# Retention and gated linear attention in one phase, with heads on row quarters of TensorE

## The reference

```
mod = silu(c) @ w_mod + b_mod;  shift, scale, gate = split(mod)
h = rms_norm(x, pre_gain) * (1 + scale) + shift
proj = h @ w_in                      # 3088 columns: attention, retention, gated linear attention (GLA)
r: retention, 4 heads of 64, chunks of 128 tokens
   sc = (q k^T) * dmask;  out = sc v + (q*q_decay) state;  state = chunk_decay*state + (k*k_decay)^T v
g: GLA, 4 heads, key width 32, value width 64, chunks of 64 tokens
   log_a = log_sigmoid(ga @ gate_w + gate_b) / 16;  b = cumsum(log_a) in the chunk
   sc[i,j] = sum_d q[i,d] k[j,d] exp(b[i,d]-b[j,d]) for j <= i
   out = sc v + (q*exp(b)) state;  state = exp(b_last)*state + (k*exp(b_last-b))^T v
r, g: rms_norm over each head, times silu of their gate columns
y = [attention, r, g] @ w_out;  x = x + gate * rms_norm(y, post_gain)
```

## Time and profile before

| what | before |
|---|---|
| median of 3 runs | 2690.21 us (2686.27 to 2691.15) |
| the profiled execution's own time | 2677.06 us |
| its span, first to last instruction | 2675.3 us |
| PE busy, share of the span | 90% |
| DVE, ACT, POOL busy | 51%, 32%, 40% |
| mean granted TensorE clock | 0.968 of full speed |

### The profile page before, as it was taken

One profiled execution on the slowest core, in us unless ns is written; L12 is line 12 of the kernel. 1 busy time (PEld: TensorE's weight loads), 2 busy tenths in 40 slices (PEclk: granted clock), 3 DMA queues, 4 the chain that ended last, 5 costly groups with the idle time before them and its releaser, 6 DMA issues.

```text
span 2675.3 us, 33460 instructions
## 1 busy us (share of the span) xinstructions
PE 2412.1 (90%) x13114; PEld 1993.8 (75%) x13114; DVE 1362.1 (51%) x2043; ACT 851.6 (32%) x1624; POOL 1076.0 (40%) x793
## 2 busy tenths in 40 slices
PE   3889689988689988888899999999899899999998
PEld 3777467777467865667799998989778667788886
DVE  4885654794654965547753352313479673210112
ACT  2224113214114156563422121211421784322222
POOL 1433326333326233232444242433544343655454
PEclk9999899999899999999999999999999999999999
DMA  7541013440022420002332232324153001222222
GB/s 247 169 146 37 1 56 91 153 155 5 1 64 65 150 56 1 1 9 91 111 103 79 83 107 87 103 67 130 36 185 98 17 1 40 63 98 99 95 95 79
DMA packets 147733, 218.95 MB, mean 82 GB/s; under 512 B 18485, under 2 KB 71125, under 8 KB 147449
## 3 DMA queue, kind: packets, MB, share of 16 engines
q1 hardware_dynamic: 147576, 216.82, 25.2%
HBM read 214.69 MB, written 2.10 MB: 81 GB/s over the span
## 4 chain that ended last, share of the span: by engine, by line
PE 51%; DVE 3%; ACT 2%; POOL 1%; issue 1%; DMA 0%; ACTq 0%; DVEq 0%; POOLq 0%; SPq 0%
PE ps L306 13%; PE ps L307 13%; PE ps L308 13%; PE ps L983 4%; PE ps L1011 3%; PE ps L1033 1%; PE ps L1030 1%; POOL h_transposed L560 1%; PE ps L1272 1%; PE ps L393 1%; DVE x_tokens L842 0%; PE ps L572 0%; DVE mod_acc_aux L366 0%; ACT att_probs_lat L1071 0%; PE ps L1267 0%
## 5 line engine op out<-in xcount | busy, mean ns | idle before, releaser
L295 POOL TENSOR_TENSOR w_lo<-w_raw,w_hi 128x1024 fp32r<-128x1024 f32 (+3 forms) x252 | 590.8, 2346 | 995.7 <-ACT w_hi L288 995.6
L288 ACT ACTIVATE w_hi<-w_raw 128x1024 fp32r<-128x1024 f32 (+3 forms) x252 | 255.7, 1016 | 1167.9 <-PE ps L308 983.8
L306 PE MATMUL ps<-w_hi,h_transposed 128*128 128x512 f32 (+3 forms) x1088 | 418.1, 384 | 57.0 <-POOL w_lo L295 26.5
L307 PE MATMUL ps<-w_lo,h_transposed 128*128 128x512 f32 (+3 forms) x1088 | 409.2, 376 | 0.0
L308 PE MATMUL ps<-w_hi,h_transposed 128*128 128x512 f32 (+3 forms) x1088 | 408.9, 376 | 0.0
L306 PE MATMUL ps<-h_transposed,w_hi 128*128 128x384 f32 (+1 forms) x1056 | 374.7, 355 | 8.1 <-POOL h_transposed L560 6.5
L307 PE MATMUL ps<-h_transposed,w_hi 128*128 128x384 f32 (+1 forms) x1056 | 373.9, 354 | 0.0
L308 PE MATMUL ps<-h_transposed,w_lo 128*128 128x384 f32 (+1 forms) x1056 | 373.9, 354 | 0.0
L366 DVE SCALAR_TENSOR_TENSOR mod_acc_aux<-w_raw,c_act,mod_acc_aux 128x512 f32<-128x512 f32 x280 | 283.4, 1037 | 41.5 <-DMA w_raw<-in_w_mod_dram 19.1
L306 PEld LDWEIGHTS ps<-w_hi,h_transposed 128*128 128x128 f32 x1088 | 213.3, 196 | 103.0 <-POOL w_lo L295 31.1
L1465 DVE TENSOR_TENSOR ffn_full<-ps,ffn_silu 128x768 f32<-128x768 f32 (+1 forms) x44 | 34.2, 819 | 430.8 <-PE ps L308 430.8
(11 more groups left out here) (312 smaller groups left out, 3634.3 us busy)
## 6 DMA issues: line engine op xcount, KB each, us to landing
w_raw<-in_ada_w_dram SPq DMA_DIRECT2D x96, 512.0 KB, 3.8
w_raw<-in_ffn_w_in_dram SPq DMA_DIRECT2D x88, 512.0 KB, 3.5
w_raw<-in_w_mod_dram SPq DMA_DIRECT2D x48, 512.0 KB, 4.5
w_raw<-in_ffn_w_out_dram SPq DMA_DIRECT2D x44, 512.0 KB, 3.5
w_raw<-in_w_in_dram SPq DMA_DIRECT2D x40, 512.0 KB, 4.2
w_raw<-in_w_out_dram SPq DMA_DIRECT2D x16, 512.0 KB, 4.9
w_raw<-in_od_w_in_dram SPq DMA_DIRECT2D x16, 512.0 KB, 3.9
mod_gain<-in_norm_g_dram SPq DMA_DIRECT2D x16, 256.0 KB, 3.9
```

The costliest lines, as they stand in the source:

```text
L288: act.activation(w_hi[:, i % 2, 0:k * n], w_raw[:, u % 4, 0:k * n], ACT.Copy).then_inc(w_hi_ready.sem, 1)
L295: pool.tensor_tensor(w_lo[:, i % 2, 0:k * n], w_raw[:, u % 4, 0:k * n], w_hi[:, i % 2, 0:k * n].bitcast(F32), ALU.subtract).then_inc(w_lo_ ...
L306: pe.matmul(acc, left[0], right[0], start=start, stop=False)
L307: pe.matmul(acc, left[0], right[1], start=False, stop=False)
```

## The change

- `Modulation`: x is loaded after the first job; a job's gain is loaded behind its fourth transfer; squares, roots, scales and the turns of six of the eight column tiles of x stand inside `Modulation`, between the turns of jobs 1 and 2; the barrier of its own for x is gone. The constants are loaded inside the w_in `Linear`, behind its second weight transfer.
- `Linear` with w_in: the rotary steps of tiles 0 and 1 stay in chunks 2 and 4, those of tiles 2 and 3 go to chunks 3 and 5.
- The decayed q and k of retention are made in the `Pieces` phase ahead of attention: 8 more transposes, two masked copies on DVE, four products on POOL.
- The 19 phases become one, `Memories`, with semaphores between single steps and one barrier at its end. Score banks 0 to 3 belong one to each head; banks 4 to 6 are used in turn by all other products. GLA's scores use rows 32h to 32h+31 of the array for head h (`tile_position`), in two halves of two heads. A level has only the later tokens as targets, so 256 columns for all four tiles instead of 512 for each; q and k are multiplied for half of the tokens; the copies take 256 columns a head. What stood in phases behind the levels (decays, updates, states, the sums of squares of retention) is put between the levels (`beside_level`). SP loads the next constants and weights when the last level's q and k are made.

```diff
-                if q == 2 and self.gain is not None:
+                u = ring_slot(sp, "mod")
+                sp.dma_start(w_raw[:, u % 4, :]...)
+                if q == 3 and self.gain is not None:
...
+                for t in range(XT):
+                    self.norm.turn(pe, t, range(6), None, t == XT - 1)
+                for job in self.jobs[2:]:
+                    job.turn(pe)
...
+            linear.beside["dve"] = {2: [rotate_columns(0, AQ, AV, 1, (0, 1))], 3: [rotate_columns(0, AQ, AV, 1, (2, 3))],
+                                    4: [rotate_columns(1, RQ, RV, 3, (0, 1))], 5: [rotate_columns(1, RQ, RV, 3, (2, 3))]}
...
+            def level_scores(self, pe, l, half):
+                if half == 0:
+                    self.wait(pe, g_ql, l + 1)
+                    self.wait(pe, g_kl, l + 1)
+                self.wait(pe, g_cp, 2 * l + half + 1)
+                for t in range(XT):
+                    for h in (2 * half, 2 * half + 1):
+                        rows = slice(32 * h, 32 * h + 32)
+                        ins = pe.matmul(ps[:, h, 64 * t:64 * t + 64], g_k[rows, l % 2, tok(t)], g_q[rows, l % 2, 64 * t:64 * t + 64],
+                                        start=True, stop=True, tile_position=(32 * h, 0))
+                ins.then_inc(g_mm.sem, 1)
...
+            def tensor(self, pe):
+                pe.matmul(self.bank(self.Z), gate_w[:, :], gaT[:, :], start=True, stop=True).then_inc(mem_made.sem, 1)
+                self.own_scores(pe, 0)
+                self.own_scores(pe, 1)
+                self.wait(pe, mem_cleared, 3)
+                for t in range(XT):
+                    self.retained(pe, t)
+                log_tok = self.open(pe, self.LOG)
+                self.wait(pe, gate_log, 1)
...
+                for t in range(XT):
+                    self.retention_out(pe, t)
+                keep_clock(pe, 2)
+                for l in range(len(LEVELS)):
+                    for half in range(2):
+                        self.level_scores(pe, l, half)
+                    if l == 0:
...
+                    if l == 1:
+                        self.update(pe, self.UPD)
+                        self.update(pe, self.UPD + 1)
...
+                    if l >= 3:
+                        keep_clock(pe, 2)
+                for t in range(XT):
+                    self.gated_out(pe, t)
+                keep_clock(pe, 16)
...
+            def beside_level(self, dve, step):
+                if step == 0: ...   # distance to the chunk's end
+                if step == 1: ...   # g_qe = gqT * f_in
+                if step == 2: ...   # g_kd = gkT * f_out
+                if step in (3, 4): ...   # keep two updates each
+                if step == 5: ...   # seven state steps
+                if step == 6: ...   # squares and sums of retention
...
+            # DVE, vector(): gate_min; keep_retained 0, 1; place_own 0, 1; log_a; keep_retained 2, 3; ret_s;
+            # then for step in range(8): distance(step), q(step-1), place(step-2, both halves), beside_level(step);
+            # then head_gate and head_sums of both results
...
+            # ACT, scalar(): gate abs, exp, ln; keep LOG, SUMS; f_in, gla_decay; keep RET_OUT 0 to 3;
+            # factor(0); f_out; factor(1), (2); keep KD; factor(3) to (5); keep OUT 0 to 3
```

More of the change, by code:

```diff
@@ L470, in __init__ @@
                 self.prime = prime
-                self.host, self.added, self.ahead = None, None, []
+                self.host, self.added, self.ahead, self.beside = None, None, [], None
                 self.T = XT + (CT if with_ctx else 0)
@@ L548, in gpsimd @@
             def gpsimd(self, pool):
-                if self.added is None:
+                if self.added is None and not self.beside:
                     for t in range(self.T):
@@ L1752, in layer_one, with rotate_columns @@
             linear = schedule[-1]
-            def rotate_columns(which, c0, c1, chunk):
+            def rotate_columns(which, c0, c1, chunk, tiles):
                 def step(eng):
@@ L1757, in step @@
                     linear.wait_copied(eng, chunk)
-                    for t in range(XT):
+                    for t in tiles:
                         x = P1[:, t, c0:c1]
@@ new lines, in update @@
+            def update(self, pe, g):
+                par, two = (g - self.UPD) // 2, (g - self.UPD) % 2
+                rows = slice(GLA_C * par, GLA_C * par + GLA_C)
+                acc = self.open(pe, g)
+                if g == self.UPD:
+                    self.wait_kept(pe, self.KD)
+                for i, t in enumerate((2 * two, 2 * two + 1)):
+                    ins = pe.matmul(acc[:, i * 256:(i + 1) * 256], g_kdt[rows, t, :], P1[rows, t, GV:GV + 256], start=True, stop=True)
+                ins.then_inc(mem_made.sem, 1)
@@ new lines, in place_own @@
+            def place_own(self, dve, half):
+                mask = c1t("levels")[:, 6 * P:7 * P].bitcast(U32).unsqueeze(1).to_broadcast([P, XT, P])
+                self.wait(dve, g_mm, half + 1)
+                if half == 0:
+                    self.wait(dve, mem_cleared, 1)
+                for h in (2 * half, 2 * half + 1):
+                    v = lambda z: z.rearrange("p (t n) -> p t n", n=P)
+                    ins = dve.copy_predicated(v(gla_a[:, h, :]), mask, v(ps[:, h, :]))
+                ins.then_inc(g_cp.sem, 1)
@@ L1989, in vector @@
+                        dve.tensor_tensor(g_q[:, l % 2].rearrange("p (b n) -> p b n", n=s), later(gqT[:, :]), later(g_exp[:, l % 2]), ALU.mult)\
                            .then_inc(g_ql.sem, 1)
[L1990 to L1999 removed]
@@ L2001, in gpsimd @@
-            def gpsimd(self, pool):
-                for step in range(len(LEVELS) + 1):
-                    l = step
-                    if l < len(LEVELS):
-                        s = LEVELS[l]
+                    if step >= 2:
+                        self.place(dve, step - 2, 0)
+                        self.place(dve, step - 2, 1)
+                    self.beside_level(dve, step)
+                self.wait(dve, g_cp, 2 * n + 2)
+                dve.wait_ge(rstd_ready.sem, self.r0 + 1)
@@ new lines, in vector @@
+                self.head_gate(dve, 0, RQ, RG, range(0, 2))
+                for two in range(2):
+                    self.wait_kept(dve, self.OUT + 2 * two + 1)
+                    ins = self.head_sums(dve, 1, GQ, range(2 * two, 2 * two + 2))
+                dve_s.chain(ins)
+                self.head_means(dve, 1)
+                self.head_gate(dve, 0, RQ, RG, range(2, XT))
+                dve.wait_ge(rstd_ready.sem, self.r0 + 2)
+                self.wait(dve, gains_ready, 1)
+                self.head_gate(dve, 1, GQ, GG, range(XT))
```

503 lines of the change are left out of this document (311 added, 192 removed).

## The result

The changed kernel took 2602.06 us (median of 4 runs, 2599.96 to 2604.27) against 2689.59 us: ratio 0.9677, 95% interval 0.9661 to 0.9692, or 87.5 us less. Faster, inside the range, 22 us above the forecast of 2580. Its profiled execution took 2599.96 us with a span of 2598.2.

What follows compares the result with a forecast made beforehand. No engine was full; steps waiting for each other over 19 barriers bound the rewritten stretches. Phases -86, pieces +2.4, start -14.5 and w_in -12 gave -110 from the 2690 median: 2580 us, range 2556 to 2616.

Steps and rivals of the forecast that it cites:

- phases: Retention and GLA stretch, end of attention to turn of mixed rows: 66 us against 109.1 a layer, 86 less in all.
- start: Before the first w_in product: earlier jobs and row work in their shadow save 14.5 us (10 to 17).
- w_in: Two w_in products: half the rotary work leaves chunks where DVE has a job, -7 and -5, together -12 us.
- One more us for TensorE's clock: In the retention and GLA phase: 1 us a layer added because PE idles 2 to 3 us several times.
- rival 1: PE at 1.2 GHz through most of the retention and GLA phase: +16 us a layer, 2612 us; chance 0.18.
- to level 0: From the barrier behind attention through log, summed logs, retention outputs and first exponential: level 0 begins at 20.6 us.
- levels: From level 0 to the last copy: DVE issues 26.0 us of work plus about 2.4 of waits, ending at 49.
- to the turn: After the last copy: GLA outputs 6.5, squares 2.1, POOL's root 3.34, eight steps 3.4, sinks and barrier 0.5 us.
- rival 2: Strided predicated copies or PE quarters in the levels cost as before: +7 us a layer, 2594 us; chance 0.14.
- Quarters side by side: In the levels, passes in different PE rows run side by side: half a level takes 0.9 us, otherwise 1.8.
- rival 3: Start and w_in products give only half their forecast gain: +13 us, 2593 us; chance 0.11.
- Rival 4: Strided predicated copies and products pay for each piece, making the kernel slower: at 35 ns 2705 us; chance 0.02.

Runs made afterwards that it cites:

- experiment 4: Kernel before with only the new start (x after first job, gains later, rows turned beside the jobs, constants in the first product): 2673.87 us, ratio 0.9939.
- experiment 3: Kernel before with only the rotary steps of tiles 2 and 3 moved to chunks 3 and 5 of w_in: 2681.7 us, ratio 0.9979.
- experiment 1: Changed kernel plus 256-column fillers: 8 before level 0's turns of decayed keys, 2 after levels 1 and 2, 5 instead of 2 after levels 3 to 5: 2582.79 us.
- experiment 12: Kernel of experiment 1 with each filler behind level 0 and later as four 64-column matmuls on all 128 rows: 2658.27 us, ratio 0.9881.
- experiments 9: Kernel of experiment 1 reordered, five fillers in the wait for retention states, retention outputs and key turns spread over levels 0 and 1 without fillers between: 2591.92 us.
- experiment 11: Reordered kernel of experiments 9 with more 256-column fillers ahead of level 0, behind the third and fourth retention outputs and levels 1 and 2: 2575.66 us, ratio 0.9588.
- experiment 6: Changed kernel with only eight 256-column fillers added ahead of the turns of the decayed keys in level 0: 2594.03 us, ratio 0.9656.

## Why the prediction was right, and where it was not

Sign and order came out; the saving was 0.8 of what I forecast. One of the signs of being wrong that I had named was met: the clock in the phase is 0.66, below 0.75. Term by term, with the second profile of before as the usual one:

| Term | Forecast, us | Measured, us | From |
|---|---|---|---|
| phases | -86 (109.1 to 66) | -68.5 (114.2, 114.5 to 79.6, 80.6) | traces |
| phases in absolute length | 2 x 66 | 160.2, so +28 | trace |
| start | -14.5 | -16.4 (-11 to -22) | experiment 4 |
| w_in | -12 | -5.6 (-1 to -10) | experiment 3 |
| pieces | +2.4 | +2.0 (8.8 to 9.6, 7.1 to 8.3) | traces |
| sum | -110 | -88.5, runs -87.5 | |

That the sum of the terms comes within 1 us of the runs is closer than the intervals of two of them allow, and so in part luck.

**The step that failed: "One more us for TensorE's clock".** I charged 1 us a layer and made the rest rival 1 at 0.18. The rival's mechanism is what happened; it asked for +16 a layer and the phase stands 14 above the forecast. Of these, experiment 1 gives back 9. I had the cause wrong as well: I read the earlier trace rows as a sign that idle time lowers the clock. It does in that place (the clock fell at 307.9, with TensorE idle from 304.4 to 313.7), but in the new phase it stays low while the engine is busy. And I held the 0.92 and 0.90 of the earlier trace rows against the rival, though the stages of before kept the clock with passes of 512 columns and fillers. In the rest of their levels, 319.0 to 349.9, TensorE was busy for 72% of the time, less than in any of the slow stretches shown above, at the full clock:

```profile
319.00:349.90 30.90, 22.38 (x50) 8.71 (x48) 28.45 (x36) 1.89 (x3) 10.84 (x6) 1.00 0.00 1
```

The Trainium skill, TensorE: Matmul & The Clock Gate, The HAM clock gate, says that the gate is set by how busy the engine has been of late. By that rule 85.3 busy us of 85.3 should run at the full clock; experiment 12 measured 0.50. In this kernel the measurement decides: the busy share of the profile doesn't tell whether the clock holds. What moved it was the number of wide passes among the narrow ones (experiments 9 and 11, 1 and 12). But the eight wide fillers of experiment 1 bring the same 2048 columns in 16 passes and 6.61 us that the narrow ones of experiment 12 bring in 64 passes and 13.92 us, so the columns and the weight loads in a us change together with the width, and no run tells them apart.

**Where the phase stands against the plan** (from its start to level 0, from there to the last copy, then to the turn):

| | Forecast | Changed | Exp. 1 | Exp. 11 |
|---|---|---|---|---|
| to level 0 | 20.6 | 24.0 | 24.0 | 19.5 |
| levels | 28.4 | 35.0 | 31.6 | 32.4 |
| to the turn | 16 + 1 | 20.7 | 15.3 | 15.3 |
| phase | 66 | 79.6 | 70.9 | 67.3 |

To level 0: the chain through logarithm and sums stood behind work that could wait; the order of experiment 11 takes 4.5 us out. A stretch of 6.8 us at half clock at the phase's start (260.2) is in all versions of the new phase and was not tried. Levels: still 3.2 over in experiment 1 and 4.0 in experiment 11, which has two retention outputs among them. VectorE's work was sized rightly there, 25.6 and 25.1 us busy against the 26.0 that I added up; it waits 6.0 and 7.4 us where I had put 2.4, 3.2 of them for level 1 behind the eight slow fillers in experiment 1, and 4.2 for the first update in experiment 11. Four copies of the last two levels take 2.42 us against 1.42 for the others. This is rival 2 in part, but only for runs of two columns and one, and it is small: all 24 copies take 10.8 us against 10.1 (their mean of 537 ns counts the time in which they overlap):

```profile
310.43 2.42 DVE L2039 COPY_PREDICATED gla_scores_t<-constants_one,ps 128x256 f32<-128x256 uint32 x4
```

Quarters side by side were right: 32 passes in 1.61 to 1.74 us at the full clock, 0.8 to 0.9 a half level, as forecast. To the turn: 16 was about right at the full clock (15.3), root 2.97 against 3.34.

**w_in**: half as much as forecast, near rival 3's size for this part. In the changed kernel's trace the products are 3.8 and 5.1 us shorter, with the other parts of the change in. In layer 0 the waits for the copies went from 8.9 to 7.1 us only the earlier trace rows, where I had asked for 4 or less; in layer 1 they went, but the waits for POOL's low parts grew from 4.7 to 10.6 us. I had named VectorE's jobs as next, and what was next was the weight split.

**Start**: right within 2 us, the first product at 46.7 (45 to 47 asked for). **The base**: a profile of the short kind set both phases at 109.1; the usual 114.2 and 114.5 gave 10 us that I had not counted, 8.3 of them from the execution and 2.1 from the window of layer 1, which I had cut short. That the miss was no larger is luck: from the usual base the same 66 us would have made the forecast about 2570, and the miss 32 us and not 22. **Rival 4** is excluded: no four copies take over 2.43 us. Its price was also summed wrongly: 504 x 4 pieces at 35 ns are 71 us a layer, so about 2720 and not 2705.

Open: why the same program fell to the low clock at 351.6 in one execution and not in another, what lowers it at the phase's start, and what it is in the wide passes that brings it back.

## What to carry to other kernels

When a stage is rewritten from few wide matmuls into many narrow ones, forecast it once at either clock, and look at the granted clock before the busy share: a TensorE that is 90% busy at 0.50 wants wide passes among the narrow, where it would wait anyway, and not fewer fillers. They have to stand all along the narrow stretch; part of them gave about half of the gain or next to nothing. And take a second profile of the kernel before: here two executions of it differed by 5.0 and 3.3 us in the two phases, and the clock there was what set them apart.

## What the runs showed of the hardware

- Stretches made up mostly of passes of 64 columns, in 32 rows or in all 128, ran at 0.50 for 47.8, 30.7 and 85.3 us with TensorE busy for 90, 99 and 100% of the time (the changed kernel, experiments 6 and 12). With more fillers of 256 columns among the same level passes, it was 1.00 over 31.1 us at 97% (experiment 11).
- A filler of 256 columns is cheaper than four of 64: at the full clock eight took 3.72 us (experiment 6) against 7.36 (experiment 12, layer 1), at half clock 6.61 (but for the last 0.7 us) against 13.92.
- A predicated copy of 256 columns out of PSUM with its target in runs of four or more took 0.36 us, in runs of two or one 0.60.
- Two VectorE steps with inputs in SBUF took longer beside GpSimd's: the distance of 512 columns took 0.68 alone and 1.20 beside GpSimd's products, the q product of 256 columns 0.41 and 1.25, in the changed kernel:

```profile
284.17 1.20 DVE L2118 SCALAR_TENSOR_TENSOR gla_distance<-gla_distance 128x512 f32<-128x512 f32 x1 [0.99 <-POOL gla_distance L2198]
...
288.60 0.68 DVE L2118 SCALAR_TENSOR_TENSOR gla_distance<-gla_distance 128x512 f32<-128x512 f32 x1
```
